# Handing half of the weight splits and the rounding of the gated products of a convolutional FFN from VectorE and ScalarE to GpSimd

## The reference

```python
u2 = rmsnorm(h, g_ffn[l])                       # (1, 256, 1024)
up = causal_dwconv(u2 @ w_up[l], ffn_conv_w[l]) + ffn_conv_b[l]   # w_up: 1024 x 5632, 3 taps
a, b = jnp.split(up, 2, axis=-1)                # 2816 each
h = h + (jax.nn.silu(a) * b) @ w_down[l]        # w_down: 2816 x 1024

def causal_dwconv(x, w):                        # y[t] = x[t]*w[2] + x[t-1]*w[1] + x[t-2]*w[0]
    K, T = w.shape[0], x.shape[1]
    xp = jnp.pad(x, ((0, 0), (K - 1, 0), (0, 0)))
    y = xp[:, K - 1:K - 1 + T] * w[K - 1]
    for k in range(K - 1):
        y = y + xp[:, k:k + T] * w[k]
    return y
```

## Time and profile before

| | |
|---|---|
| median of the runs | 1696.11 us |
| the profiled execution's own time | 1696.11 us |
| its span | 1694.0 us |
| TensorE busy | 1610.8 us, 95% |
| VectorE busy | 886.9 us, 52% |
| ScalarE busy | 781.2 us, 46% |
| GpSimd busy | 94.6 us, 6% |
| up stage, first and last matmul | 474.2 us to 602.8 us |
| down stage | 602.9 us to 666.4 us |

### The profile page before, as it was taken

The page is one execution under the profiler, slowest core; times in us unless marked ns, Lnnn a source line. Parts: engine busy times, 40 slices in busy tenths (PEclk is TensorE's granted clock), DMA queues, the critical chain, the costliest instruction groups (busy, mean ns, idle before and its releaser), DMA issues.

```text
span 1694.0 us, 25812 instructions
## 1 busy us (share of the span) xinstructions
PE 1610.8 (95%) x10186; PEld 1351.4 (80%) x10186; DVE 886.9 (52%) x1793; ACT 781.2 (46%) x2001; POOL 94.6 (6%) x45
## 2 busy tenths in 40 slices
PE   5999899999989998899999999999999989999997
PEld 4698778887889997578888888888888865787775
DVE  2257476455278865765656555555652034655501
ACT  4164443453267765655554555555552125444410
POOL 2144000000000000000000000000000001221100
PEclk8999999999999999899999999999999989999989
DMA  7364222122445554121111112111212223222210
GB/s 297 104 254 145 96 100 99 50 75 82 143 160 189 175 188 161 50 75 51 51 57 69 51 50 75 51 51 51 75 51 75 100 99 124 100 81 94 75 50 25
DMA packets 26152, 167.30 MB, mean 99 GB/s; under 512 B 3632, under 2 KB 6064, under 8 KB 6448
## 3 DMA queue, kind: packets, MB, share of 16 engines
q1 hardware_dynamic: 24848, 164.53, 27.9%
q10 hardware_dynamic: 1184, 1.11, 0.2%
HBM read 164.58 MB, written 1.05 MB: 98 GB/s over the span
## 4 chain that ended last, share of the span: by engine, by line
PE 89%; DVE 6%; ACT 3%; DMA 1%; issue 1%; POOL 0%; DVEq 0%; SPq 0%; ACTq 0%; POOLq 0%
PE bank L945 15%; PE bank L627 8%; PE bank L643 8%; PE bank L645 7%; PE bank L644 7%; PE bank L960 4%; PE bank L781 3%; PE bank L727 3%; PE bank L1091 3%; PE bank L657 2%; PE bank L1107 2%; PE bank L973 2%; PE bank L666 2%; PE bank L1190 2%; PE bank L1189 1%; PE bank L1084 1%
## 5 line engine op out<-in xcount | busy, mean ns | idle before, releaser
L945 PE MATMUL bank<-arena,ring 128*128 128x272 f32 x1024 | 291.3, 409 | 5.4 <-DVE arena L2150 4.6
L945 PEld LDWEIGHTS bank<-arena,ring 128*128 128x128 f32 x1024 | 180.5, 192 | 45.6 <-issue 10.1
L561 DVE TENSOR_TENSOR w_lo<-ring,w_hi 128x1024 fp32r<-128x1024 f32 x102 | 128.1, 1258 | 119.6 <-ACT w_hi L1287 118.7
L1287 ACT ACTIVATE w_hi<-ring 128x1024 fp32r<-128x1024 f32 x138 | 145.2, 1055 | 76.1 <-PE bank L645 49.4
L561 POOL TENSOR_TENSOR w_lo<-ring,w_hi 128x1024 fp32r<-128x1024 f32 x36 | 92.9, 2582 | 1014.1 <-ACT w_hi L1287 1014.1
L1255 ACT ACTIVATE arena<-bank 128x272 f32<-128x272 f32 (+2 forms) x161 | 65.8, 410 | 169.6 <-PE bank L945 52.9
L643 PE MATMUL bank<-u_hi,w_hi 128*128 128x256 f32 (+1 forms) x480 | 137.9, 287 | 6.4 <-DVE u_lo L2099 6.1
L645 PE MATMUL bank<-u_hi,w_lo 128*128 128x256 f32 (+1 forms) x480 | 137.7, 287 | 0.0
L644 PE MATMUL bank<-u_lo,w_hi 128*128 128x256 f32 (+1 forms) x480 | 137.5, 286 | 0.0
L627 PE MATMUL bank<-arena,ring 128*128 128x272 f32 (+1 forms) x480 | 111.6, 392 | 2.0 <-ACT arena L1255 0.9
L627 PEld LDWEIGHTS bank<-arena,ring 128*128 128x128 f32 x480 | 92.6, 193 | 19.1 <-ACT arena L1255 1.3
(11 more groups left out here) (409 smaller groups left out, 3565.6 us busy)
## 6 DMA issues: line engine op xcount, KB each, us to landing
ring<-wstream SPq DMA_DIRECT2D x151, 1024.0 KB, 4.9
con<-consts SPq DMA_DIRECT2D x1, 2520.0 KB, 15.2
h<-xT SPq DMA_DIRECT2D x1, 1024.0 KB, 6.0
arena<-wlora ACTq DMA_DIRECT2D x1, 1024.0 KB, 4.9
outT<-h SPq DMA_DIRECT2D x2, 512.0 KB, 2.9
arena<-decays SPq DMA_DIRECT2D x2, 384.0 KB, 5.4
arena<-decays SPq DMA_DIRECT2D x1, 256.0 KB, 5.6
vec<-vecs SPq DMA_DIRECT2D x1, 252.5 KB, 5.8
```

The source lines that it names most:

```text
L561: ops.tensor_tensor(lo, whole, hi.bitcast(F32), ALU.subtract).then_inc(S(signal), 1)
L945: ins = nc.tensor.matmul(b[:, 0:T2], weights(), x, start=k == 0, stop=k == DT - 1)
L1287: nc.scalar.activation(hi, whole, ACT.Copy).then_inc(S("w_hi_ready"), 1)
```

## The change

The remainders of odd units go from VectorE to GpSimd throughout the feed-forward net; VectorE keeps the even ones (`split_even`). GpSimd also rounds the product (a copy with a change of type, L2435 of the changed kernel) and makes its low part (L2437). Tap 2 and the bias go from ScalarE to VectorE: ScalarE now only copies an output to `up`, with the general helper `take` (L1255), and VectorE does six convolution instructions a step, two of them `tensor_scalar` (L2089) and four `scalar_tensor_tensor` (L2091). The product of step m-1 now comes behind the taps of step m on VectorE, and silu of step m-1 behind the copies of step m on ScalarE. The rounding of unit 46 that stood ahead of the last silu is no longer there; unit 46 is rounded behind the table load.

```diff
--- before.py
+++ after.py
@@ -1508,35 +1508,17 @@
                 act.wait_ge(S("upc_ready"), m + 1)
                 nc.scalar.activation(prod[:, m, :], upc[:, 2 * (m % 2), :], ACT.Silu).then_inc(S("up_silu"), 1)
 
-            def take_up(m, j):
-
-                i = taken_n[0]
-                taken_n[0] += 1
-                s = 2 * (m % 2) + j
-                act.wait_ge(S("proj_done"), i + 1)
-                nc.scalar.activation(up[:, s, 2:], bank[i % 2][:, 0:T1], ACT.Copy)
-                nc.scalar.activation(upc[:, s, :], bank[i % 2][:, 0:T1], ACT.Identity, scale=V("ffn_conv_w", 2 * 44 + j * FT + m),
-                                     bias=V("ffn_conv_b", j * FT + m)).then_inc(S("proj_taken"), 1)
-
-            def round_prod(m):
-
-                act.wait_ge(S("ffn_prod"), m + 1)
-                nc.scalar.activation(prod_hi[:, m, :], prod[:, m, :], ACT.Copy).then_inc(S("prod_hi_ready"), 1)
-
             for m in range(FT):
+                s = 2 * (m % 2)
+                if m >= 2:
+                    act.wait_ge(S("upc_ready"), m - 1)
                 split_hi(first_units + 2 * m + 3)
+                take(up[:, s, 2:])
+                split_hi(first_units + 2 * m + 4)
+                take(up[:, s + 1, 2:])
                 if m >= 1:
                     up_silu(m - 1)
-                if m >= 2:
-                    act.wait_ge(S("ffn_prod"), m - 1)
-                take_up(m, 0)
-                split_hi(first_units + 2 * m + 4)
-                take_up(m, 1)
-                if m >= 1:
-                    round_prod(m - 1)
-            split_hi(first_units + 2 * FT + 3)
             up_silu(FT - 1)
-            round_prod(FT - 1)
             root_table()
             for b in range(DT):
                 split_hi(down_units(b))
@@ -1873,14 +1855,6 @@
                     split_lo(dve, V_, 2 * evens[0], "w_lo_even")
                     evens[0] += 1
 
-            both = [first_units]
-
-            def split_both(upto):
-
-                while both[0] < min(upto, ffn_end):
-                    split_lo(dve, V_, both[0], ("w_lo_even", "w_lo_odd")[both[0] % 2])
-                    both[0] += 1
-
             split_even(1)
             for t in range(DT):
                 dve.wait_ge(S("u_tile"), t + 1)
@@ -2062,7 +2036,7 @@
 
                 for b in range(DT):
                     if base:
-                        split_both(down_units(b))
+                        split_even(down_units(b))
                     dve.wait_ge(S("proj_taken"), first + b + 1)
                     V_.tensor_tensor(h[:, b, META:], h[:, b, META:], outs[:, b, :], ALU.add).then_inc(S("h_tile"), 1)
                     if base and 1 <= b < DT - 1:
@@ -2089,7 +2063,7 @@
                 if t:
                     ins.then_inc(S("norm_mix"), 1)
 
-            split_both(first_units + HALVES)
+            split_even(first_units + HALVES)
             add_to_h(conv, 68 + 16, 0)
             norm([u[:, t, 0:T1] for t in range(DT)], [h[:, t, META:] for t in range(DT)],
                  [V("g_ffn", t) for t in range(DT)], T1, "u_tile")
@@ -2099,34 +2073,30 @@
                 V_.tensor_tensor(u_lo[:, t, :], u[:, t, 0:T1], u_hi[:, t, :].bitcast(F32), ALU.subtract).then_inc(S("u_lo_ready"), 1)
 
             V_.memset(up[:, :, 0:2], 0.0).then_inc(S("up_zeroed"), 1)
-            def lower_prod(m):
-
-                dve.wait_ge(S("prod_hi_ready"), m + 1)
-                V_.tensor_tensor(prod_lo[:, m, :], prod[:, m, :], prod_hi[:, m, :].bitcast(F32), ALU.subtract).then_inc(S("prod_split"), 1)
-
             for m in range(FT + 1):
-                split_both(first_units + 2 * m + 3)
+                if m < FT:
+                    s = 2 * (m % 2)
+                    split_even(first_units + 2 * m + 3)
+                    dve.wait_ge(S("proj_taken"), 92 + 2 * m + 2)
+                    if m >= 2:
+                        dve.wait_ge(S("up_silu"), m - 1)
+                        dve.wait_ge(S("ffn_prod"), m - 1)
+                    for tap in (2, 0, 1):
+                        for j in range(2):
+                            w = V("ffn_conv_w", tap * 44 + j * FT + m)
+                            src, dst = up[:, s + j, tap:tap + T1], upc[:, s + j, :]
+                            if tap == 2:
+                                ins = V_.tensor_scalar(dst, src, w, V("ffn_conv_b", j * FT + m), ALU.mult, ALU.add)
+                            else:
+                                ins = V_.scalar_tensor_tensor(out=dst, in0=src, scalar=w, in1=dst, op0=ALU.mult, op1=ALU.add)
+                        if tap != 1:
+                            link(ins)
+                    ins.then_inc(S("upc_ready"), 1)
                 if m >= 1:
                     dve.wait_ge(S("up_silu"), m)
                     dve.wait_ge(S("upc_ready"), m)
                     s = 2 * ((m - 1) % 2)
                     V_.tensor_tensor(prod[:, m - 1, :], prod[:, m - 1, :], upc[:, s + 1, :], ALU.mult).then_inc(S("ffn_prod"), 1)
-                if m >= 2:
-                    lower_prod(m - 2)
-                if m < FT:
-                    split_both(first_units + 2 * m + 4)
-                    dve.wait_ge(S("proj_taken"), 92 + 2 * m + 2)
-                    s = 2 * (m % 2)
-                    for tap in range(2):
-                        for j in range(2):
-                            w = V("ffn_conv_w", tap * 44 + j * FT + m)
-                            src, dst = up[:, s + j, tap:tap + T1], upc[:, s + j, :]
-                            ins = V_.scalar_tensor_tensor(out=dst, in0=src, scalar=w, in1=dst, op0=ALU.mult, op1=ALU.add)
-                        if tap == 0:
-                            link(ins)
-                    ins.then_inc(S("upc_ready"), 1)
-            lower_prod(FT - 1)
-            evens[0] = ffn_end // 2
             n0 = 92 + 2 * FT
             add_to_h(down, n0, DT)
             V_.tensor_tensor(gain2, vec[:, VOFF["g_final"]:VOFF["g_final"] + DT], vec[:, VOFF["norm_pre_2"]:VOFF["norm_pre_2"] + DT], ALU.mult)
@@ -2457,6 +2427,18 @@
             nc.gpsimd.memset(T0, 0.0).then_inc(S("rw_zeroed"), 1)
             pool.wait_ge(S("rw_zeroed"), 3)
 
+            for m in range(-1, FT + 1):
+                if m < FT:
+                    split_lo(pool, nc.gpsimd, first_units + 2 * m + 3, "w_lo_odd")
+                if m >= 1:
+                    pool.wait_ge(S("ffn_prod"), m)
+                    nc.gpsimd.tensor_copy(prod_hi[:, m - 1, :], prod[:, m - 1, :]).then_inc(S("prod_hi_ready"), 1)
+                    pool.wait_ge(S("prod_hi_ready"), m)
+                    nc.gpsimd.tensor_tensor(prod_lo[:, m - 1, :], prod[:, m - 1, :], prod_hi[:, m - 1, :].bitcast(F32), ALU.subtract)\
+                        .then_inc(S("prod_split"), 1)
+            for i in range(first_units + 2 * FT + 3, ffn_end, 2):
+                split_lo(pool, nc.gpsimd, i, "w_lo_odd")
+
             pool.wait_ge(S("proj_done"), 92 + 2 * FT + DT)
             nc.gpsimd.memset(lo[64:128, 0, :], 0.0).then_inc(S("lo_zeroed"), 1)
             pool.wait_ge(S("lo_zeroed"), 1)
```

## The result

The changed kernel takes 1721.82 us, the median of 4 runs (1721.46 to 1722.8), against 1695.78 us before (4 runs): a ratio of 1.0155, 95% interval 1.0138 to 1.0173. The forecast was 1721 us. Its profiled execution has a span of 1720.1 us, 26.1 us more than before.

The account below looks back on a forecast made before the run. TensorE's rate bounds the up stage; VectorE and GpSimd in series exceed it by 1.2 us over 22 steps, 26.4 us, less 4.7, leaving 21.7. With 3 us for the passage, 24.7 on 1696.11 gives 1721 us, range 1704 to 1738.

Parts of the forecast that it names:

- The bound: Up stage: runs at TensorE's own rate, 5.76 us a step; relieving side engines can bring at most 0.9 us.
- The exclusion: Up stage: VectorE and GpSimd do not run beside each other; whichever comes second stands still, about 2.17 us per remainder.
- rival A: Up stage: tensor_scalar does not exclude GpSimd, cast 0.30 and subtraction 0.54 us; step 6.26 us, time 1705 us; 20%.
- Rival C: Up stage: engine waits fall in idle time, stage stays at 126.7 us, only unit 46 late; 1697 us; 6%.
- The sum of a step: Up stage: VectorE 3.8, GpSimd remainder 2.17, cast 0.40, subtraction 0.60 in series: 6.96 us against TensorE's 5.76.
- the 4.7 us taken off for the first steps and the lead: Up stage: 2.7 us for two steps lacking products or casts, 2.0 us of lead, off 26.4 us, leaving 21.7.
- one sign of being wrong: Up stage: TensorE's waits naming even remainders would refute; expected were about 20 waits of 1.1 us for odd ones.
- The passage: Up stage to down stage: unit 46, rounded behind silu and table load, comes late; 3 us, ends 2 and 4.5.
- The chain from the end of the up stage to unit 46: Passage: copy, taps, GpSimd remainder, silu, table load, rounding, remainder take 9.0 us against 5.76, 3.2 us too late.
- The down stage proper: Down stage: VectorE and GpSimd hold 4.2 us of 5.76 per unit pair; costs nothing, at most 2 us.
- Rival B: Up stage: GpSimd waits for whole runs of VectorE instructions; step 7.6 to 7.7 us, time 1735 us; 20%.
- Rival D: Up stage: stops lower TensorE's clock, 0.12 us a matmul becomes 0.24, 127 us more, above 1800 us; 4%.

Follow-up runs that it names:

- e8: The kernel before, with only tap 2 and bias moved from ScalarE to VectorE, GpSimd idle: 1693.04 us.
- e10: The kernel before, with only rounding and low part of the products moved to GpSimd: 1693.62 us.
- e11: The changed kernel with all remainders back on VectorE and unit 46 rounded ahead of the last silu again: 1693.24 us.
- e9: The kernel before, with only odd remainders on GpSimd and ScalarE rounding the odd unit ahead of silu and copies: 1696.96 us.
- e1: The changed kernel, but GpSimd rounds and lowers the product of two steps ago instead of the last one: 1726.97 us.
- e3: The changed kernel with rounding of the product back on ScalarE and its low part back on VectorE: 1719.47 us.
- e4: The changed kernel with all remainders back on VectorE, GpSimd only rounding and lowering products: 1693.41 us.
- e6: The changed kernel, but GpSimd writes zeros three times (memsets) instead of making odd remainders in the feed-forward net: 1709.2 us.
- e2: The changed kernel with tap 2 and bias back on ScalarE, without VectorE's two tensor_scalar: 1711.15 us.
- e7: The kernel before, with only the odd remainders of the feed-forward net moved to GpSimd: 1707.49 us.
- e5: The changed kernel with unit 46 rounded ahead of the last silu again, as before the change: 1718.39 us.

## Why the prediction was right

**The bound.** TensorE's rate bound the stage with almost nothing to win: e8, e10 and e11 relieve ScalarE and move work about, and none is clear of the kernel before.

**The exclusion.** It was read from the earlier trace rows and carries the result. The `tensor_scalar`, for which no row stood, excludes GpSimd: a remainder that starts at 554.97 on GpSimd makes one of them, started at 555.08, take 2.48 us, and 19 of the 44 do. With that the milder rival A falls. Rival C is refuted by the 150.3 us of the up stage; e9 shows what it would have needed, a sum under 5.76 us and an order without a ring.

**The sum of a step.** 6.96 us forecast, 6.94 measured. Cast and subtraction, bounded at 0.30 to 0.60 and 0.54 to 0.85 us, are 0.40 us and 0.73 us as recorded (0.70 start to start), against 0.40 and 0.60 taken, and the odd remainder with what is left of the `tensor_scalar` takes 2.60 us (561.90 to 564.50) against 2.17 + 0.54: errors of 0.1 to 0.2 us that cancel, so the match to 0.02 us is luck as much as bounds. The up stage lost 21.7 us, as forecast; its first stop comes 25.7 us into the stage, some four steps of no loss, which is what the 4.7 us taken off for the first steps and the lead amount to.

**The shape was off, and one sign of being wrong appeared.** TensorE was to stop about 20 times for 1.1 us, ahead of odd units only, and waits that name the even remainders were listed as a sign that the prediction is wrong. They make 17 of the 35 stops. Units start at 557.56, 561.01, 564.50 and 567.95 us, about 3.5 us apart where 2.88 is undisturbed. What failed is the place of the remainders in the step: the odd one was to be ready some 4 us after the even one, and is 3.5 us after it (560.86 and 564.35), because no tap is done ahead of the subtraction; and the even one had been taken to be in time, but comes 3.5 us after the odd one, later than the 2.88 us of a unit. So the same 1.2 us of a step fall on both units. The sum of a step, which gives the time, does not depend on how it is divided. Whether two short stops instead of a longer one also spared the clock was not tried; in the up stage it stayed at 1.00.

**The passage was mis-sized.** It was to cost 3 us and cost 5.4. The wait for unit 46 is 3.09 us, close to what was worked out, but two errors stand behind it. The chain from the end of the up stage to unit 46 was to take 9.0 us and takes 9.65 (623.46 to 633.11), mostly in the taps: from 623.60 to 628.85 they take 5.25 us and not 2.3 + 2.17, since GpSimd's subtraction stands ahead of them as well as its remainder. And the lateness of unit 45, some 0.5 us, is a loss of the passage too. Late units make 9.65 - 5.76 = 3.9 us. The rest is the clock, for which the prediction's sum had no term here. Behind the stop the windows read (TensorE, weight loads, VectorE, ScalarE, GpSimd, clock):

```profile
629.50:633.00 3.50, 0.52 (x5) 0.32 (x3) 1.56 (x2) 3.49 (x5) 2.15 (x5) 1.00 0.45 185
633.00:638.00 5.00, 4.89 (x28) 4.89 (x29) 3.14 (x3) 1.87 (x5) 2.30 (x1) 0.66 0.30 85
638.00:644.00 6.00, 6.00 (x52) 6.00 (x52) 1.23 (x1) 2.57 (x4) 2.41 (x1) 1.00 0.45 150
```

28 matmuls in 5 us where 41 would start: 1.6 us. The down stage proper costs nothing, as forecast: behind unit 46 TensorE waits for no remainder. Together the stages lost 21.7 + 5.4 = 27.1 us instead of 24.7. The time is 26.0 us above the kernel before, since this execution's up stage began 1.0 us earlier; and as the kernel before measured 0.3 us less this time, 1721.82 us lies only 0.8 us from the forecast. That closeness is luck.

**Rival B**, GpSimd waiting for whole runs as in the earlier trace rows: it did not in this stage. The cast starts at 559.79 us, 0.15 us behind VectorE's remainder (559.64), waits for the rest of that one, 0.93 us, and gets in ahead of the taps; that wait is already in the sum. B's own sum was off as well: with cast and subtraction at their high ends the step is 6.96 + 0.45 = 7.4 us, not 7.6 to 7.7. **Rival D**, the clock: from 482 to 602 us it was 1.00. In e1, e3 and the passage it came true in part, behind single long stops, for about 5 us each, but not behind two of e1's; and the lower level costs 0.21 us a matmul there, not the 0.24 of D's price.

What stays open: why e3 falls into a pattern of few long stops and the changed kernel into many short ones. That GpSimd enters between product and low part is seen in e3's timeline, and in e1 it enters between the last tap and the product; that this is the reason was not tried. The 2 to 3 us by which e4, e8 and e11 lie under the kernel before are inside the spread of its runs and are not claimed.

## What to carry to other kernels

For the instructions of this net (two operands from SBUF, or `tensor_scalar`, against GpSimd's subtraction) VectorE and GpSimd work like one engine: before giving work to an idle GpSimd, add up what both hold in a period and compare it with the bound of the stage; their separate busy shares (3.8 and 3.4 of 5.76 us here) say nothing. Then look for a ring through the instruction that is stopped: with the same sum, the order of one rounding on ScalarE made 10 us of difference. One long stop of TensorE can cost more than the same time in short ones, because the clock may fall behind it: here by 1.6 us and more behind most stops of over 2 us, and behind none of the 35 short ones.

## What the runs showed of the hardware

- An instruction of VectorE with two SBUF operands, or `tensor_scalar`, started just behind a GpSimd instruction that reads SBUF, lasts until that one's end: 2.48 to 2.60 us for instructions of 0.40 to 0.42 us. Against GpSimd's memset, `tensor_scalar` is stopped and the two-operand form is not (e6).
- A GpSimd instruction that comes while one of VectorE runs waits for it: the cast takes 1.33 us instead of 0.40 in 20 of 22 steps. It then often gets in ahead of VectorE's next one even where that follows at once (in e4 the cast ends at 562.13 us between two remainders that together take 2.55 us instead of the 2.36 undisturbed), but not always: at the kernel's start it waited for nine, and in e11 four casts took 2.46 us.
- GpSimd's cast of 128x256 takes 0.40 us and its subtraction 0.73 us, where a quarter of the remainder of 128x1024 would be 0.60.
- Stops of TensorE of 0.3 to 0.7 us, 35 of them in the up stage, left the granted clock at 1.00. Behind stops of 2.1 to 3.5 us it read 0.50 to 0.67 over the next 5 us, in e2, e3, e6, e7, the changed kernel and five times in e1, but 1.00 behind two stops of 2.7 us in e1; behind one of 1.59 us (e5) it stayed at 1.00.
